# First attention round: queries and keys interleaved by quarters of x, two quarters of x transposed by VectorE

## The reference, cut to what matters

```python
h = x                                            # (1, 256, 2048)
y = rmsnorm(h, sb_norm[0])                       # row scale from mean(h*h), gain per column
q, k, v = jnp.split(y @ sb_w_qkv[0], 3, axis=-1) # w_qkv: 2048 x 6144
# 16 heads of 128: scores q k^T, stick-breaking weights, times v, then @ w_o, added to h
```

## Time and profile before

| | |
|---|---|
| time, median of 3 runs | 2109.99 us (2109.95 to 2110.03) |
| profiled execution: time / span | 2109.97 us / 2108.1 us |
| busy: TensorE / VectorE / ScalarE | 2097.1 / 1407.9 / 973.2 us |
| busy share of the span | 99% / 67% / 46% |
| mean granted TensorE clock | 0.999 |
| VectorE busy in the first 77.09 us | 53.47 us |
| DMA, mean over the span | 191 GB/s |

### The profile page before, as it was taken

One profiled execution on the slowest core, in us unless ns is written; L12 is line 12 of the kernel. 1 busy time (PEld: TensorE's weight loads), 2 busy tenths in 40 slices (PEclk: granted clock), 3 DMA queues, 4 the chain that ended last, 5 costly groups with the idle time before them and its releaser, 6 DMA issues.

```text
span 2108.1 us, 27412 instructions
## 1 busy us (share of the span) xinstructions
PE 2097.1 (99%) x9429; PEld 1738.5 (82%) x9429; DVE 1407.9 (67%) x1759; ACT 973.2 (46%) x1107; POOL 15.9 (1%) x29
## 2 busy tenths in 40 slices
PE   9999999999999999999999999999999999999998
PEld 7888888888888888888888888888888888888886
DVE  6787787766666676665555587857666676664453
ACT  6555555544444444444445444554444444444443
POOL 1000000000000000000000000000000000000000
PEclk9999999999999999999999999999999999999999
DMA  8655555666666666555566665566666666655554
GB/s 268 182 169 169 178 175 172 193 195 193 192 195 191 192 195 190 196 192 194 195 191 199 186 205 186 186 195 193 195 189 194 194 191 195 189 196 195 191 195 144
DMA packets 207131, 402.47 MB, mean 191 GB/s; under 512 B 12305, under 2 KB 12897, under 8 KB 206689
## 3 DMA queue, kind: packets, MB, share of 16 engines
q1 hardware_dynamic: 206352, 398.51, 61.2%
q0 software_dynamic: 688, 3.18, 0.4%
q10 hardware_dynamic: 32, 0.01, 0.0%
HBM read 399.55 MB, written 2.10 MB: 191 GB/s over the span
## 4 chain that ended last, share of the span: by engine, by line
PE 99%; ACT 0%; DVE 0%; issue 0%; POOLq 0%; POOL 0%; DVEq 0%; ACTq 0%
PE acc L1040 32%; PE acc L1041 32%; PE acc L1042 32%; PE tp L1251 0%; PE tp L1050 0%; PE tp L1100 0%; PE tp L1090 0%; PE tp L1113 0%; PE tp L1091 0%; PE tp L1092 0%; PE tp L1114 0%; PE acc L1077 0%; PE tp L1112 0%; PE acc L1292 0%; PE acc L1290 0%
## 5 line engine op out<-in xcount | busy, mean ns | idle before, releaser
L623 DVE TENSOR_TENSOR w_lo<-raw,w_hi 128x1024 fp32r<-128x1024 f32 x750 | 915.7, 1224 | 584.1 <-ACT w_hi L333 580.5
L333 ACT ACTIVATE w_hi<-raw 128x1024 fp32r<-128x1024 f32 x750 | 794.5, 1061 | 945.8 <-PE acc L1042 942.4
L1040 PE MATMUL acc<-w_hi,xT 128*128 128x512 f32 x2048 | 799.6, 390 | 0.7 <-DVE xT L642 0.5
L1042 PE MATMUL acc<-w_hi,xT 128*128 128x512 f32 x2048 | 797.1, 389 | 0.0
L1041 PE MATMUL acc<-w_lo,xT 128*128 128x512 f32 x2048 | 797.0, 389 | 0.0
L1042 PEld LDWEIGHTS acc<-w_hi,xT 128*128 128x128 f32 x2048 | 384.4, 188 | 80.3
L1040 PEld LDWEIGHTS acc<-w_hi,xT 128*128 128x128 f32 x2048 | 384.4, 188 | 80.1 <-issue 0.9
L1041 PEld LDWEIGHTS acc<-w_lo,xT 128*128 128x128 f32 x2048 | 384.5, 188 | 78.4
L1040 PE MATMUL acc<-w_hi,hid_hi 128*128 128x512 f32 x944 | 367.6, 389 | 0.0
L1042 PE MATMUL acc<-w_hi,hid_lo 128*128 128x512 f32 x944 | 367.3, 389 | 0.0
L1041 PE MATMUL acc<-w_lo,hid_hi 128*128 128x512 f32 x944 | 367.3, 389 | 0.0
(11 more groups left out here) (120 smaller groups left out, 504.1 us busy)
## 6 DMA issues: line engine op xcount, KB each, us to landing
raw<-in_ffn_w_gate_up SPq DMA_DIRECT2D x352, 512.0 KB, 4.5
raw<-in_ffn_w_down SPq DMA_DIRECT2D x176, 512.0 KB, 3.7
raw<-in_sb_w_qkv SPq DMA_DIRECT2D x95, 512.0 KB, 4.4
raw<-in_gm_w_in SPq DMA_DIRECT2D x64, 512.0 KB, 4.3
raw<-in_sb_w_o SPq DMA_DIRECT2D x32, 512.0 KB, 4.2
raw<-in_gm_w_o SPq DMA_DIRECT2D x32, 512.0 KB, 4.0
h<-in_x SPq DMA_DIRECT2D x3, 512.0 KB, 8.6
gain_bc<-in_gm_v_norm POOLq DMA_DIRECT2D x1, 1024.0 KB, 8.5
```

The costliest lines, as they stand in the source:

```text
L333: nc.scalar.activation(w_hi[:, p % RING], raw[:, p % RING], ACT.Copy).then_inc(hi_ready, 1)
L623: nc.vector.tensor_tensor(w_lo[:, p % RING], raw[:, p % RING], w_hi[:, p % RING].bitcast(f32), ALU.subtract).then_inc(lo_ready, 1)
L1040: nc.tensor.matmul(dst, hi[:, kt, rs], w_hi[:, p % RING, k], start=(kt == 0), stop=False)
L1042: last = nc.tensor.matmul(dst, lo[:, kt, rs], w_hi[:, p % RING, k], start=False, stop=(kt == K - 1))
```

## The change

In round 0 the 16 pieces of queries and keys change their order (`FIRST`): queries 0 to 3, keys 0 to 3, queries 4 and 5, keys 4 and 5, queries 6 and 7, keys 6 and 7; the values follow as before. The matmuls and the accumulators are the same. Piece 8 in this order is thus the queries' fifth, the first that needs x's third quarter (tiles 8 to 11), and piece 12 the first that needs the fourth.

TensorE transposes only the first two quarters of x. The third and fourth are turned by VectorE in blocks of 32 x 32 (new `turn_x` on VectorE), 16 instructions for each quarter, straight from x into the same PSUM tiles: the third in iterations 2 to 5 (four instructions each), the fourth in iterations 6 to 10 (2, 2, 4, 4, 4). ScalarE copies the third quarter's tiles after the weight copy of iteration 6, VectorE makes their low halves after the subtraction of iteration 7; for the fourth quarter both come in iteration 11. x's last quarter is loaded ahead of piece 5, thus behind the load of piece 4 and its wait for a free buffer, instead of ahead of piece 4.

The squares move to iterations 2, 3, 5 and 8, the mean square to 9, the row transposes behind piece 9, the evacuation of the queries to iteration 13 (after piece 13). Queries and keys are turned by VectorE in iterations 15 to 23 (`QK_FIRST`) instead of 9 to 15 and 17 to 23. Rounds 1 to 3 are as before.

```diff
+    FIRST = [(sec, p) for ps in (range(LATE - 2), range(LATE - 2, LATE), range(LATE, PD)) for sec in range(2)
+             for p in ps] + [(2, p) for p in range(PD)]
+    QK_FIRST = {15: (0, (0, 1)), 16: (0, (2, 3)), 17: (0, (4, 5)), 18: (0, (6, 7)), 19: (1, (0, 1)), 20: (1, (2,)),
+                21: (1, (3, 4)), 22: (1, (5, 6)), 23: (1, (7,))}
...
+                    if t in (2, 3, 5):
+                        c = {2: 1, 3: 2, 5: 3}[t]
+                        load_x(slice(c * CH, (c + 1) * CH), x_loaded[c])
+                    load(AT_QKV, 0, 3 * PD, t, src, p * KP)
...
-                    if not with_attention and t in (1, 2):
-                        x_tiles_gained(range((t + 1) * TC, (t + 2) * TC), 3 + t)
                     ahead(AT_QKV, j, 3 * PD, t)
                     if not with_attention:
-                        if 3 <= t < 3 + ND:
-                            c = t - 3
+                        if t in (6, 11):
+                            c = 2 if t == 6 else 3
+                            x_tiles_gained(range(c * TC, (c + 1) * TC), 2 + c)
+                        if t in (2, 3, 5, 8):
+                            c = (2, 3, 5, 8).index(t)
...
+            def turn_x(c, units):
+                if 0 in units:
+                    dve.wait_ge(x_loaded[c], 16)
+                for n in units:
+                    for b in (2 * (n % 2), 2 * (n % 2) + 1):
+                        a = n // 2
+                        last = nc.vector.transpose(
+                            tp[c % 2][b * Q:(b + 1) * Q, :].rearrange("p (k r q t) -> p k r q t", k=TC, r=RT,
+                                                                       q=4)[:, :, :, a],
+                            h[a * Q:(a + 1) * Q, :, c * CH:(c + 1) * CH].rearrange("p r (k q c) -> p k r q c", k=TC,
+                                                                                   q=4)[:, :, :, b])
+                if 7 in units:
+                    last.then_inc(n_turned[0], 1)
...
                     ahead(AT_QKV, j, 3 * PD, t)
-                    if t == 6 and not with_attention:
-                        mean_square(0, ND)
+                    if not with_attention:
+                        if 2 <= t < 6:
+                            turn_x(2, (2 * t - 4, 2 * t - 3))
+                        if t == 7:
+                            x_tiles_low(range(2 * TC, 3 * TC))
+                        if 6 <= t < 11:
+                            turn_x(3, ((0,), (1,), (2, 3), (4, 5), (6, 7))[t - 6])
+                        if t == 9:
+                            mean_square(0, ND)
+                        if t == 11:
+                            x_tiles_low(range(3 * TC, 4 * TC))
...
+            def first_round():
+                for t, (sec, p) in enumerate(FIRST):
+                    if sec == 2 and p == 0:
+                        pe.wait_ge(q_out, 1)
+                    piece(AT_QKV, 0, 3 * PD, t, sec, p * KP, KD, xT_hi, xT_lo, first=sec == 0)
+                    if t == 0:
+                        turn_x(1)
+                    if t == 9:
+                        pe.wait_ge(rows_loaded, 4 * 16)
+                        turn_rows(tp[0][:, 0:4 * KD], rows, 4 * KD)
```

More of the change, by code:

```diff
@@ L60, in hybrid_trunk @@
     LATE = PD - TC // KP
+    FIRST = [(sec, p) for ps in (range(LATE - 2), range(LATE - 2, LATE), range(LATE, PD)) for sec in range(2)
+             for p in ps] + [(2, p) for p in range(PD)]
+    QK_FIRST = {15: (0, (0, 1)), 16: (0, (2, 3)), 17: (0, (4, 5)), 18: (0, (6, 7)), 19: (1, (0, 1)), 20: (1, (2,)),
+                21: (1, (3, 4)), 22: (1, (5, 6)), 23: (1, (7,))}
+    QK_ROUND = {PD * (1 + second) + 1 + n: (second, units) for second in range(2)
+                for n, units in enumerate(((0, 1), (2,), (3,), (4,), (5,), (6,), (7,)))}
     SBO_PAIR = [(c, p) for c in range(2) for p in range(LATE)] + [(c, p) for p in range(LATE, PD) for c in range(2)]
@@ L220, in _, with qkv_body @@
             qkv = sb_w_qkv[0].rearrange("(k p) n -> p k n", p=P)
-            def qkv_body(j, first):
+            def first_round():
+                for t, (sec, p) in enumerate(FIRST):
+                    src = qkv[:, :, sec * D:sec * D + CH]
+                    if t == 0:
+                        sp.dma_start(raw[:, 0, 0:KP // 2], src[:, 0:KP // 2, :]).then_inc(w0_half_loaded, 16)
+                        load_x(slice(0, CH // 2), x_loaded[0])
+                        sp.dma_start(raw[:, 0, KP // 2:KP], src[:, KP // 2:KP, :]).then_inc(raw_loaded[0], 16)
+                        load_x(slice(CH // 2, CH), x0_rest_loaded)
+                        continue
+                    if t in (2, 3, 5):
+                        c = {2: 1, 3: 2, 5: 3}[t]
+                        load_x(slice(c * CH, (c + 1) * CH), x_loaded[c])
+                    load(AT_QKV, 0, 3 * PD, t, src, p * KP)
+            def qkv_body(j):
                 for sec in range(3):
@@ L225, in qkv_body @@
                     for p in range(PD):
[L226 to L233, removed]
                         load(AT_QKV, j, 3 * PD, sec * PD + p, src, p * KP)
@@ L254, in ffn @@
                             load(AT_DOWN[layer], i, 2 * PF, cc * PF + p, src, p * KP)
-            qkv_body(0, True)
+            first_round()
             with sp.Fori(1, ND) as j:
-                qkv_body(j, False)
+                qkv_body(j)
             w_o = sb_w_o[0].rearrange("(k p) n -> p k n", p=P)
@@ L438, in qkv_round @@
                 for t in range(3 * PD):
-                    if not with_attention and t in (1, 2):
-                        x_tiles_gained(range((t + 1) * TC, (t + 2) * TC), 3 + t)
                     ahead(AT_QKV, j, 3 * PD, t)
                     if not with_attention:
-                        if 3 <= t < 3 + ND:
-                            c = t - 3
+                        if t in (6, 11):
[3 more added lines that the diff above has]
+                            c = (2, 3, 5, 8).index(t)
                             if c:
                                 act.wait_ge(n_sq[0], c)
+                                act.wait_ge(x_loaded[c], 16)
+                            else:
+                                act.wait_ge(x0_rest_loaded, 16)
                             squares(0, c, h[:, :, c * CH:(c + 1) * CH])
-                        if t == 6:
+                        if t == 10:
                             act.wait_ge(rows_turned, 2)
@@ L451, in qkv_round @@
                                                  ACT.Copy).then_inc(cols_ready, 1)
-                    if t == PD - 1:
+                    if t == (PD - 1 if with_attention else PD + LATE - 1):
                         if not with_attention:
                             act.wait_ge(n_rstd[0], 1)
-                        q_or_k(j, 0, q_s, q_out, PD)
+                        q_or_k(j, 0, q_s, q_out, t + 1)
                     if t == 2 * PD - 1:
@@ L692, in qkT_lows, with turn_qk @@
                                         high[:, :, :].bitcast(f32), ALU.subtract).then_inc(qkT_ready, 1)
-            def turn_qk(j, t):
-                second = t > 2 * PD
+            def turn_x(c, units):
[11 more added lines that the diff above has]
+                    last.then_inc(n_turned[0], 1)
+            def turn_qk(j, second, units):
                 src, dst, ready = (k_s, k_t, k_out) if second else (q_s, q_t, q_out)
-                units = ((0, 1), (2,), (3,), (4,), (5,), (6,), (7,))[(t - 1) % PD]
-                if t % PD == 1:
+                if 0 in units:
                     dve.wait_ge(ready, j + 1)
@@ L705, in turn_qk @@
                             src[a * Q:(a + 1) * Q, :, :].rearrange("p r (k q c) -> p k r q c", k=TC, q=4)[:, :, :, b])
-                if t % PD == PD - 1:
+                if 7 in units:
                     last.then_inc(qk_turned, 1)
@@ L763, in qkv_round @@
                 for t in range(3 * PD):
-                    if t in (1, 2) and not with_attention:
-                        x_tiles_low(range((t + 1) * TC, (t + 2) * TC))
                     ahead(AT_QKV, j, 3 * PD, t)
-                    if t == 6 and not with_attention:
-                        mean_square(0, ND)
+                    if not with_attention:
[9 more added lines that the diff above has]
+                            x_tiles_low(range(3 * TC, 4 * TC))
                     if with_attention:
                         attention(j - 1, t)
-                    if t > PD and t % PD:
-                        turn_qk(j, t)
+                    qk = QK_ROUND if with_attention else QK_FIRST
+                    if t in qk:
+                        turn_qk(j, *qk[t])
                     if t == 3 * PD - 1:
@@ L1059, in turn_x @@
                 pe.wait_ge(x_loaded[c], 16)
[L1060 to L1063, removed]
+                pe.wait_ge(cols_ready, 1)
                 turn(tp[c % 2], h[:, :, c * CH:(c + 1) * CH]).then_inc(n_turned[0], 1)
@@ L1125, in attention, with first_round, qkv_round @@
                         scores(g, i)
```

(20 more changed lines are left out.)

## The result

| | before | after |
|---|---|---|
| median of 8 runs | 2110.03 us (2109.95 to 2110.15) | 2116.48 us (2115.73 to 2117.05) |
| profiled execution: time / span | 2109.97 / 2108.1 us | 2116.57 / 2114.9 us |
| second round's first matmul | 77.09 us | 83.85 us |

The ratio is 1.0031 (95% interval 1.0022 to 1.0039): 6.5 us slower, inside the predicted range and 1.0 us above the predicted 2115.5.

What follows compares the result with a forecast made beforehand. TensorE, busy 99%, was taken to bound the kernel; 1.6 us ahead, stalls of 4.7 and 2.2 and two restarts of 0.13 sum to +5.6 on 2109.97, so 2115.5 us, range 2113.2 to 2117.0.

Steps and rivals of the forecast that it cites:

- What bounds the kernel: TensorE, busy 99% of the span; whatever the first round gains or loses reaches the end unshortened.
- The start and the gain: First round: piece 2 starts at 15.11 us; two quarters off TensorE free 1.8 us; piece 7 ends 1.6 us ahead.
- Four iterations of 3.01 and 3.17: VectorE's iterations 2 to 5, a subtraction and four transposes each: 3.01 + 3 x 3.17 us, ending at 31.87.
- The anchor: VectorE's iteration 2 starts at 19.35 us, after weight piece 5 lands at 18.2, 5.5 us after issue.
- The clock: Rival: TensorE's clock falls in the stall ahead of piece 8; upper end +6.9 us, 2116.8; chance 0.20.
- the sum: Second round's first matmul 5.6 us later (-1.6, +4.7, +2.2, two restarts of 0.13), giving 2115.5 us.
- unharmed or unfelt: Case of two stalls in the first round without felt clock loss: 2114.2 to 2116.0 us, chance 0.60.
- The second stall: TensorE ahead of piece 12 waits 2.2 us for VectorE's low tile, ready at 49.9 us.
- All hidden: Rival: block transposes of 0.2 us or less, so piece 8 would not wait; 2108.4 us, chance 0.05.
- Only one stall: Rival: VectorE regains 2.2 us after piece 8, piece 12 unhindered; +3.3 us, 2113.3; chance 0.13, with both stalls shorter.
- lower end: Block transposes out of x on VectorE at 0.44 us instead of 0.46, 18 of them: -0.3 us.

Runs made afterwards that it cites:

- Run 9: Changed kernel, but TensorE transposes x's third quarter and VectorE only the fourth, two transposes in each of iterations 2 to 9: 2108.92 us against 2109.93.
- run 3: Changed kernel plus 20 matmuls of zeros on TensorE in the stall ahead of piece 8: 2115.48 us, ratio 1.0027 to the kernel before.
- Run 5: Changed kernel with only 8 of the 16 block transposes of x's third quarter (output not the reference's): 2111.53 us against 2109.93 for the kernel before.
- run 4: Changed kernel, but VectorE makes the third quarter's low tiles ahead of subtraction 10 instead of behind it: 2114.98 us, ratio 1.0026 to the kernel before.
- run 6: Changed kernel, but TensorE transposes the third quarter again and VectorE turns only the fourth, in iterations 6 to 10: 2110.51 us against 2109.93.
- run 2: Changed kernel with only the load of x's last quarter moved back ahead of piece 4's load: 2116.57 us, ratio 1.0032 to the kernel before.
- run 7: Changed kernel, but VectorE turns both quarters one iteration earlier (1 to 4, 6 to 9), tiles following at once: 2113.74 us against 2109.93.
- run 8: The kernel of run 7 plus 16 matmuls of zeros on TensorE ahead of piece 12: 2112.11 us against 2109.91 for the kernel before.

## Why the prediction was right, and where it was off

- **What bounds the kernel.** Right. The second round's first matmul moved by 6.76 us and the span by 6.8.
- **The start and the gain.** Right: piece 2 at 15.12 (15.11 predicted), piece 7's last matmul at 31.35. Run 9 measured one quarter off TensorE as 1.0 us, for 0.92.
- **Four iterations of 3.01 and 3.17.** Right in sum: 12.42 us for 12.52. A transpose out of x takes 0.457 us (447 to 466 ns, all 32), as rows 4 have it. The greater distance between x's rows costs nothing.
- **The anchor** (where VectorE's chain begins). 0.4 us off: weight piece 5 landed 5.9 us after its issue instead of 5.5, so subtraction 5 began at 19.77, not 19.35. The hand-over to ScalarE took 0.01 instead of 0.22, which gave back half. Piece 8 started at 36.51, for 36.25. From subtraction 5 to piece 8 it is 16.74 us in the changed kernel and in run 3 alike (36.34 less 19.60), whenever that load lands: the start of VectorE's chain hangs on a DMA landing. I take this for the source of the spread that run 3 kept. Run 5 speaks for it: in its slowest execution, 1.1 us above its median, subtraction 5 began 1.1 us later than in run 3. It was not tested by itself.
- **The clock.** This is the term that was mis-sized: the sum has it at nothing, and it cost 1.0 us. I took the case in which it is unharmed or unfelt for the likeliest, at 0.60 and up to 2116.0, and the one that came, at 0.20, for 2116 to 2117. It fell. It shows in piece 8's pace, 12 matmuls in 41.41 - 36.51 = 4.9 us instead of 2.8 (run 3), in weight copy 12 and so in the 1.26 us that VectorE waited for it; piece 12 started at 51.09 instead of 49.9. Run 3 put its price at 1.0 us: the mechanism that I gave for it (most swallowed by piece 12's wait, the rest by way of weight copy 12, 1.3 us) was the one that ran. With the clock kept, the measured 2115.48 is the predicted 2115.5; that they agree so closely is luck, since its executions lie between 2114.98 and 2116.02. The profiled one (2115.17) has piece 8 0.1 us later and piece 12 0.2 us earlier than predicted.
- **The second stall.** Right as a mechanism (runs 4 to 6). Its size was 2.2 us predicted; read by starts as there, it is 1.94 with the clock kept (an idle row of 1.78) and 1.06 in the changed kernel (0.90), where the slow piece 8 used up some of it.
- **The rivals.** "All hidden" fell with the price of a transpose, 0.457 us. "Only one stall" fell: the second stands alone in run 6. The Trainium skill (TensorE: Matmul & The Clock Gate, "Why this matters for your kernels") advises against idle gaps above some 3 us between bursts. The profiled executions agree with it: 5.00 (run 2), 4.77 (the changed kernel), 3.55 (run 7) and 3.30 us (run 4) of idling let the clock fall, 1.78 us and less did not; no run has a gap between 1.78 and 3.30. The figure of the Trainium skill (VectorE: DVE Perf Modes, "The three transpose paths"), 311 ns for a bf16 block of 128 x 128, is not what float32 costs here: 16 x 0.457 us for eight such blocks is 0.91 us each.
- **Two slips of counting.** Weight copy 12 is ready at 40.5 by the prediction's own terms (39.10 + 0.26 + 1.11), not at 40.7; the measured row is 39.40 + 1.06 in run 3. And its lower end counts 18 transposes at 0.44, where 30 lie on the chain to piece 12, 16 ahead of the hand-over to ScalarE and 14 behind the low tiles (-0.6, not -0.3). Neither enters the sum.

The rule for the whole: in the changed kernel VectorE has 3.1 us of work per piece where TensorE has 2.72. Two transposes per piece (2.2 us) are hidden (run 9). Four are hidden only as long as VectorE's lead of three pieces lasts: in run 7 the third quarter cost no wait and the fourth did. At two per iteration both quarters would take 16 iterations, and run 9 starts in iteration 2 and needs its tiles in iteration 10, so there are not enough pieces; that is worked out, no run tried it.

## What to carry to other kernels

Moving work off the engine that bounds is worth only what it cost there (here 0.9 us a quarter), and it is free only while the taker's work per step stays below the bounding engine's step or its lead covers the difference; add it up step by step, from the landing that lets the taker begin. VectorE was busy only 67% of the span and still became the bound from 20 to 51 us. And a stall is priced with its echo: ask how long TensorE idles, whether its clock will fall, and whether anything behind the stall waits anyway and swallows the slow matmuls.

## What the runs showed of the hardware that was not expected

- The clock does not fall at a fixed time. It fell 2.4 us after the last matmul's end in the changed kernel, sooner than in the earlier trace rows (2.9 us or more), 3.6 us in run 7, 3.8 in run 4 and 5.3 in run 2. In these last three TensorE had already resumed when it fell, by 0.1, 0.5 and 0.3 us: the stall was over and its first matmuls ran at full pace. It came back after 4.5 us of work in the changed kernel (41.0 less 36.5), and after 3.5 to 3.9 us in the three.
- So the same stall has no fixed price. In run 7, with its 3.55 us, two executions took 2111.9 and 2112.2 us at a mean granted clock of 0.999, six 2113.3 to 2113.9 at 0.998, two 2114.6 and 2115.2 at 0.997. Only one of them was profiled; the two fastest have the time of run 8, in which the clock did not fall.
- Matmuls of zeros keep the clock at 1.00 as well as others do (runs 3 and 8).
